# An attention decoder step: key and query mean squares as 32-row strips through a DRAM scratch, and a new order of bulk loads, on one core

## What is computed

```python
def rms_norm(x, gain):
    xf = x.astype(jnp.float32)
    xf = xf * lax.rsqrt(jnp.mean(xf * xf, axis=-1, keepdims=True) + RMS_EPS)
    return (xf * gain.astype(jnp.float32)).astype(x.dtype)

k = rms_norm(k.reshape(bsz, t, B_HEADS, B_DH), k_norm)
q = rms_norm(q.reshape(bsz, t, B_HEADS, B_DH), q_norm)

s = jnp.einsum('bqhd,bkhd->bhqk', qi, k_all).astype(jnp.float32) * scale
logits = jnp.where(mask, s + (c_q[..., :, None] - c_t[..., None, :]), -jnp.inf)
p = jax.nn.softmax(logits, axis=-1)
o = jnp.einsum('bhqk,bkhd->bqhd', p.astype(v_all.dtype), v_all)
return x + (o * jax.nn.silu(gate)) @ w_o
```

## Time and profile before

| what | value |
|---|---|
| median of 3 runs | 1516.23 us (1515.57 to 1516.42) |
| the profiled execution, its own time | 1516.44 us |
| its span, first to last instruction | 1514.6 us |
| mean granted clock of TensorE | 0.996 |
| busy: PE, DVE, ACT, POOL | 1479.3, 991.3, 678.2, 419.9 us |
| DMA moved | 300.53 MB, mean 198 GB/s |

### The profile page before, as it was taken

One profiled execution on the slowest core, in us unless ns is written; L12 is line 12 of the kernel. 1 busy time (PEld: TensorE's weight loads), 2 busy tenths in 40 slices (PEclk: granted clock), 3 DMA queues, 4 the chain that ended last, 5 costly groups with the idle time before them and its releaser, 6 DMA issues.

```text
span 1514.6 us, 23379 instructions
## 1 busy us (share of the span) xinstructions
PE 1479.3 (98%) x8437; PEld 1090.5 (72%) x8437; DVE 991.3 (65%) x1987; ACT 678.2 (45%) x1380; POOL 419.9 (28%) x335
## 2 busy tenths in 40 slices
PE   7999999999999999999999999999999999989998
PEld 6888888888888875446777777777777777754443
DVE  6868696877868684126377677758677676748321
...
GB/s 268 192 240 97 292 105 260 147 190 200 150 239 99 299 155 108 102 64 128 61 124 197 251 217 305 178 279 210 280 215 248 260 229 294 185 324 315 238 134 58
DMA packets 290505, 300.53 MB, mean 198 GB/s; under 512 B 25863, under 2 KB 247295, under 8 KB 290391
## 3 DMA queue, kind: packets, MB, share of 16 engines
...
## 4 chain that ended last, share of the span: by engine, by line
PE 84%; DVE 6%; ACT 5%; DMA 2%; issue 2%; SPq 1%; POOL 0%; DVEq 0%; POOLq 0%
PE psum L2134 42%; PE psum L2158 7%; PE psum L2646 7%; PE psum L2446 4%; PE psum L2472 4%; PE psum L2211 3%; PE psum L2097 2%; PE psum L2504 2%; PE psum L2406 2%; ACT psum L1274 1%; ACT psum L1283 1%; PE psum L2281 1%; PE psum L2222 1%; PE psum L2297 1%; PE psum L2299 1%
## 5 line engine op out<-in xcount | busy, mean ns | idle before, releaser
L2134 PE MATMUL psum<-arena 128*128 128x252 f32 (+1 forms) x3472 | 811.4, 384 | 2.2 <-DVE arena L1451 2.2
L2134 PEld LDWEIGHTS psum<-arena 128*128 128x128 f32 x3472 | 640.8, 190 | 124.0 <-issue 23.1
L949 POOL TENSOR_TENSOR arena<-arena 128x1024 f32<-128x1024 f32 x64 | 158.2, 2472 | 374.2 <-DMA arena<-k_pages 368.8
L1451 DVE TENSOR_TENSOR arena<-arena,psum 128x252 f32<-128x252 f32 (+1 forms) x310 | 128.8, 416 | 160.5 <-PE psum L2134 155.7
L2646 PE MATMUL psum<-arena 128*128 128x512 f32 x256 | 115.6, 604 | 4.5 <-DMA arena<-o_heads 2.9
L2158 PE MATMUL psum<-arena 128*128 128x512 f32 x256 | 113.0, 594 | 0.1
L1024 ACT COPY arena<-psum 128x252 f32<-128x252 f32 (+1 forms) x124 | 46.2, 373 | 139.5 <-PE psum L2134 139.4
L2646 PEld LDWEIGHTS psum<-arena 128*128 128x128 f32 x256 | 47.6, 192 | 63.2 <-issue 60.7
L2158 PEld LDWEIGHTS psum<-arena 128*128 128x128 f32 x256 | 47.5, 190 | 57.4 <-issue 56.5
L1087 ACT ACTIVATE arena<-arena 128x1024 f32<-128x1024 f32 x48 | 50.7, 1056 | 84.6 <-DVE arena L1497 84.2
L1274 ACT ACTIVATE psum<-psum,arena 128x640 f32<-128x640 f32 (+3 forms) x64 | 58.9, 921 | 59.9 <-DVE arena L1798 59.9
...
## 6 DMA issues: line engine op xcount, KB each, us to landing
k_pages<-in_cache_k SPq DMA_DIRECT2D x64, 512.0 KB, 6.5
v_pages<-in_cache_v SPq DMA_DIRECT2D x64, 512.0 KB, 7.2
arena<-k_pages SPq DMA_DIRECT2D x64, 512.0 KB, 5.3
arena<-v_pages SPq DMA_DIRECT2D x64, 512.0 KB, 6.8
arena<-in_w_in_a SPq DMA_DIRECT2D x32, 512.0 KB, 6.9
arena<-in_x_prompt SPq DMA_DIRECT2D x16, 512.0 KB, 7.5
arena<-in_w_kv SPq DMA_DIRECT2D x16, 512.0 KB, 6.6
arena<-in_w_in_b SPq DMA_DIRECT2D x16, 512.0 KB, 7.6
```

Of the source, the lines that this page charges most:

```text
L949: pool.tensor_tensor(k_ring[:, m % 2], k_ring[:, m % 2], q_all[:, m % S:m % S + 1, :].broadcast_to([P, PAGES, P]), ALU.mult).then_inc(kq_m ...
L1451: dve.tensor_tensor(out, more, bank[n % 2][:, 0:size(u)], ALU.add).then_inc(of.by_dve, 1)
L2134: ins = pe.matmul(bank[n % 2][:, 0:size(u)], w[:, k, :], x[:, k, :], start=(k == 0 and r in (0, 1, 3, 4)), stop=(k == HK - 1), skip_group_ ...
```

## The change

For each of k and q, `means` now makes four matmuls of 32 rows by 258 columns (W4): the slice bones[:, 48:80] is 16 columns of one head and 16 of the other, and quarter n of the columns goes to partitions 32n to 32n + 31 of bank 7. So an item holds all 1032 columns as four strips in one bank. ACT takes Ln of 128 x 258 and then Exp of the same (`rs_strips`). SP stores one partition of each strip, one row for each head of the pair (`rs_out`, two DMAs into rs_rows), and loads each head's row broadcast to that head's 64 partitions, k and q side by side in sq (`rs_in`, two DMAs). Both norms wait for both loads. Three semaphores of the heads' strips are shared with the new use.

The order on SP changes: `k_in(m + 3)`, `v_in(p, 0, 0, 1)`, the two weight loads and others move between a row's stores and its load; `rs_out` and `rs_in` stand ahead of row 6's stores; in pair 6 the early operands of the last pair stand between the stores and the load of row 7. On DVE the norms go behind `row_max(p, 7)`, scores of pages and the scalings of w_k and w_q change places. On PE, in the last pair, `y_part` of (1, 0, 3) moves ahead of `weighted(p - 1, 3)`, and `turn_num(p - 1, 0)` moves behind `kq_n(2)`.

```diff
     def means(q):
-        return [(f"m{y}{i}", q) for y in "kq" for i in range(3)]
+        return [("mk", q), ("mq", q)]
...
+            def rs_out(q):
+                sp.wait_ge(strips_set, OUT_STRIPS + 2 * (q + 1))
+                sp.wait_ge(rs_done, 16 * OUT_STRIPS + 32 * q)
+                for x in range(2):
+                    src = sq_both[16 * x:P:32].rearrange("p (y n) -> p y n", y=2)[:, :, 0:W4]
+                    sp.dma_start(rs_rows[x].rearrange("y (s n) -> s y n", n=W4), src).then_inc(strips_stored, 16)
+
+            def rs_in(q):
+                sp.wait_ge(strips_stored, 16 * OUT_STRIPS + 32 * (q + 1))
+                for x, rows in enumerate(HEAD):
+                    sp.dma_start(sq_both[rows], rs_rows[x].rearrange("y n -> (y n)").partition_broadcast(DH)).then_inc(rs_done, 16)
+
+            rs_out(0)
+            rs_in(0)
...
+            def ob_early(p):
+                sp.wait_ge(max_done, 2 * TT * (p + 1))
+                w_ob_in(early_b, 2)
+                sp.wait_ge(s_done, scored(p, TT - 1, 1))
+                for h in range(2):
+                    sp.dma_start(o_y[h], o_dram[h]).then_inc(early_b, 16)
+
             def pair(p):
...
                 store_row(p, 4)
+                k_in(m + 3)
                 load_row(p, 4)
-                k_in(m + 3)
                 store_row(p, 5)
+                if p:
+                    v_in(p, 0, 0, 1)
                 load_row(p, 5)
-                if p:
-                    v_in(p, 0, 0, 1)
                 k_in(m + 4)
+                rs_out(p + 1)
+                rs_in(p + 1)
                 store_row(p, 6)
-                load_row(p, 6)
                 sp.wait_ge(b_units.done, kq_b(p + 1, 14))
...
+                load_row(p, 6)
                 k_in(m + 5)
                 store_row(p, 7)
-                k_in(m + 6)
-                load_row(p, 7)
+                if p + 2 == PAIRS:
+                    ob_early(p)
+                    load_row(p, 7)
+                    k_in(m + 6)
+                else:
+                    k_in(m + 6)
+                    load_row(p, 7)
...
-            def rs_ln(q, y, *ns):
...
+            def rs_strips(q, y):
+
+                n = items.at("m" + "kq"[y], q)
+                act.wait_ge(items.done, n)
+                act.activation(sq[y][:, 0:W4], bank[7][:, 0:W4], ACT.Ln, bias=eps).then_inc(items.taken, 1)
+                act.wait_ge(items.taken, n)
+                act.activation(sq[y][:, 0:W4], sq[y][:, 0:W4], ACT.Exp, scale=-0.5).then_inc(strips_set, 1)
...
             def norm(q, y):
 
-                dve.wait_ge(rs_done, 2 * q + y + 1)
+                dve.wait_ge(rs_done, 16 * OUT_STRIPS + 32 * (q + 1))
...
                 if p:
                     weigh(p - 1, 0)
                     score(m - 4)
-                    score(m - 3)
                 vg_add(p, 10)
                 turn_v(p, 0)
+                row_max(p, 1)
+                vg_add(p, 11)
+                vg_add(p, 12)
                 if nxt:
                     scale_w(dve, w_k, gain_kv, p + 1, w_k_loaded, w_k_scaled)
                     scale_w(dve, w_q, gain_b, p + 1, w_q_loaded, w_q_scaled)
-                row_max(p, 1)
-                vg_add(p, 11)
-                vg_add(p, 12)
+                if p:
+                    score(m - 3)
                 vg_add(p, 13)
...
                     score(m - 2)
+                kq(1)
+                if p:
+                    score(m - 1)
                     smp_sum(p - 1, 0)
-                kq(1)
...
                 if p:
-                    score(m - 1)
                     tops(p - 1, 1)
...
+                row_max(p, 7)
+                fin(p, 2)
                 if nxt:
                     norm(p + 1, 0)
-                row_max(p, 7)
+                vg(5)
                 if nxt:
                     norm(p + 1, 1)
-                fin(p, 2)
-                vg(5)
...
+            def means(q, y):
+                dst = open_item("m" + "kq"[y], q)
+                pe.wait_ge(sq_done, 2 * q + y + 1)
+                for n in range(4):
+                    ins = pe.matmul(dst[32 * n:32 * n + 32, 0:W4], bones[:, DH - 16:DH + 16], sq[y][:, n * W4:(n + 1) * W4],
+                                    start=True, stop=True, skip_group_check=True)
+                ins.then_inc(items.done, 1)
...
                 kq_n(0)
+                last((0, 0, 3), (1, 0, 3))
                 if p:
                     weighted(p - 1, 3)
                 kq_n(1)
-                last((0, 0, 3))
...
-                last((1, 0, 3))
                 weighted(p, 0)
```

99 lines of the change are left out of this document (30 added, 69 removed).

## The result

The changed kernel takes **1529.76 us** (median of 4 runs, 1527.99 to 1534.5), the kernel before beside it 1516.33: a ratio of 1.0094, 95% interval 1.0077 to 1.011. It is slower by 13.4 us where 24.0 less were forecast, and outside the range. The profiled execution is the slowest of the four, 1534.5 us, and its span is 1532.8.

A forecast was written before the change was run, and what follows sets the result against it. PE was taken as the bound, busy 1479.3 of 1514.6 us. 19.2 + 2.1 - 2.8 + 3.5 + 2.0 = 24.0 us off the profiled execution's 1516.4 gave 1492.4 us, with an 8-in-10 range of 1486 to 1504.

The forecast's parts named there:

- Strips: PE's mean matmuls in each pair but the last: 0.68 us per group, gain 2.75 us per pair, 19.2 us in all.
- product 7's old wait: PE's 0.21 us wait per pair for DVE's addition, expected to go; counted in DVE's reordering, 1.4 us in all.
- The first set: Means ahead of the first pair: six matmuls at 3.5 us become 1.4, gain 2.1 us.
- if the norms are in time: Condition on the 2.1 us gain ahead of the first pair; seven products, some 12 us, lie behind the second mean.
- The round trip: Strips stored and broadcast back by SP and DMA: 0.4 us of PE wait per pair, -2.8 us (0 to 1.5 x 7).
- slower: Rival, 4%: the two broadcasts land one after the other at 7.5 us each; 52 us more, 1544.
- late strips: Rival, 20%: loads queue ahead of the strips; PE waits 1.9 us at product 7 in 7 pairs; 10.5 more, 1503.
- DVE's order: Earlier score on DVE removes row 4's wait for turn_v (2.1 us) and product 7's wait (1.4): +3.5 us.
- The price: Weight scalings move behind additions 11 and 12 on DVE, ending with 0.2 us of slack before PE wants them.
- If late, by tenths: Claim that DVE's moved scalings and POOL's sums are tight but not late, or late only by tenths of a us.
- Last pair: Earlier operands and y parts remove 8.0 us of waits and slow clock; +2.0 us kept (bounds -2 and +5).

The follow-up runs named there:

- fourth experiment: Changed kernel without the strips' stores and broadcasts, so keys and queries are not normed with their means: 1506.26 us, ratio 0.9927.
- fifth experiment: Changed kernel with k_in(m+3) back behind row 4's load and without the strips' stores and broadcasts: 1500.35 us, ratio 0.9897.
- sixteenth experiment: Changed kernel, k_in(m+3) back, k_in(m+4) behind four split broadcasts, norms waiting by halves (1510.12 us); on it, first pair's weight scalings back ahead of row_max(p, 1): 1506.66 us.
- tenth: Changed kernel with k_in(m+3) back behind row 4's load (1517.83 us), plus SP's old order of the last pair's early operands, PE's order still changed: 1527.76 us.
- fourteenth: Changed kernel with k_in(m+3) back behind row 4's load (1517.83 us), plus both SP's and PE's old order in the last pair: 1516.35 us.

## Why the prediction was wrong

**Strips: mechanism right.** 0.57 us to the next start, and 0.2 before them, together 0.77 against 0.68 forecast. Rows 6 to the next pair take 24.69 without the trip (fourth experiment) for 27.07, that is 2.4 us a pair for the 2.75 forecast, although 0.2 of it is product 7's old wait, which the forecast had in another term. What is missing is the wait of 0.41 us for ACT's copy and the 0.1 more of each group. I had counted soft of row 6 as "some 0.2 us later", but not that the four products had been pulled together ahead of the copy. The first set: pair 0 started 1.2 us earlier in the fourth experiment's trace and 2.5 in the fifth's, for 2.1; its condition, "if the norms are in time", failed with the trip.

**The round trip: the failed step.** "I take 0.4 us of wait per pair: -2.8 us (bounds 0, and 1.5 x 7)". It measured 23.5 us. Three of its parts were short, counted in pair 3 from the pair's start. The strips' store went out at +64.1 for +62.2 (the strips themselves were set only at +63.7, since the collision and rows 4 to 5 had held PE up, and SP came free at +64.0). Its landing took 5.1 us, for "between 1.1 and 4": the bound came from head 0, in an almost empty queue, though the earlier trace rows showed the DMA engines 0.78 busy. And the broadcasts, 1.06 MB, landed 8.4 us after the first was issued, where the sum had 4.8 to 7.5. That part is not the load's: ahead of pair 0 they took 9.0. I had priced them by head 0's load, whose packets of 4096 bytes took 0.19 us on average; those of 8256 bytes took 0.52 ahead of pair 0, and not twice 0.19. The end is +78.7, where +74.7 was to be free and the rival *slower* to decide from +78.5. It lies between *late strips* (+76.6, 20%), which had the reason right, the bulk ahead of the store, and *slower* (+82.5, 4%), which had the broadcasts slow, but one after the other: they landed 6.4 and 7.8 us after their issues, side by side. PE then waited 1.8 and 0.5 us, less than such a landing would have cost by my sum, since it came to product 7 at +78.6 and not at +76.4: 1.33 of that is the collision, 0.41 the copy, 0.45 rows 4 to 5. Taking the trip away gave back 2.4 to 2.6 us in pairs 2 to 4 and 3.6 to 4.2 in pairs 1, 5 and 6, between the two rivals (1.9 and 7.8), and in pairs 5 and 6 a part of it is the clock that fell behind the wait. Beside it stood losses that I did not have.

**The page: not in the sum.** k_in(m+3) ahead of load_row(4) was in the diff and had no term and no rival. It cost 12 us with the trip and 5.9 without. I looked at it as bytes in a queue; what it moves is the time of a POOL instruction.

**DVE's order: half right.** The wait of scores of row 4 for turn_v went, and rows 2 to 4 take 21.98 us for 22.48 where nothing else interferes (in three of pairs 1 to 6; the other three take 0.5 to 1.7 more): at most 6 x 0.5 = 3.0, for the 2.1 of this part of the term. The other 1.4, product 7's wait for its addition, went too, as the fifth experiment's trace shows. The price was read in pair 4, with 0.2 us of slack; in the first pair, where nothing of a pair before stands ahead of product 1, it is 3.2 us late. "If late, by tenths" failed there, and the sixteenth experiment gave back 3.5 us.

**Last pair: mechanism right, undone by the clock.** No wait for block_rows and o_heads, full clock in that stretch, 3.37 us for smp_out instead: all as forecast. c_hi was issued 2.7 us later in the pair, for the 2.0 of the forecast, and DVE idled 2.86 us for it; scores of row 5 still came 1.6 us earlier in the pair than before, for 2 forecast. But PE had just waited 2.11 and 1.48 us and then ran at a granted clock of 0.50: scores of row 5 and the y part took 6.97 us for 4.17. These 2.8 us are more than the gain. Such a clock was in the forecast's lower bound alone (-2). The tenth and fourteenth experiments bear out that the move is worth nothing; none takes the clock away by itself.

**The account.** 37.4 us lie between forecast and result: 20.7 the trip beyond its 2.8, 5.9 the page without the trip, some 3 the first pair, 2 the last pair, 2.6 the copy and the dearer groups. The first two are differences of medians and hold what the clock lost with them. Some 3 stay unexplained. Rows 4 to 5 vary by up to 1.3 us from pair to pair in all kernels, and I have not followed that; and terms read from one trace need not add up to medians (the profiled execution is 4.7 us above its median in the changed kernel, 4.7 below in the fifth experiment).
